# Two transformer blocks in one kernel: the triangular inverse masked after its products and turned out of PSUM, and the output gates as seven quarter products

## The chip, the cores and the metric

One core of a Trainium2 chip, float32 throughout. The metric is the device time in microseconds of one execution. The program is written for the engines directly: each of TensorE (PE), VectorE (DVE), ScalarE (ACT), GpSimd (POOL) and SyncE (SP, which issues the loads) has a list of its own, in an order written out by hand, and waits on counters that the other engines raise.

## The reference

x is 256 tokens of 1024 channels. Block 1 (a mixer of four branches and a gated feed-forward) is not touched. Block 2 projects its normalised input and computes, per channel pair-block of 128,

```python
c_val, c_gate, c_og, ts, r_og, g_conv, g_rwkv = jnp.split(p, SPLITS, axis=-1)
y_conv = _conv_branch(c_val, c_gate, c_og, ...)
y_rwkv = _rwkv7_branch(ts, r_og, ...)
m = jax.nn.sigmoid(g_conv) * y_conv + jax.nn.sigmoid(g_rwkv) * y_rwkv
```

The recurrent branch is a scan over tokens, sixteen heads of 64 channels:

```python
sk = jnp.einsum('bhvk,bhk->bhv', state, kk_t)
state = (state * w_t[:, :, None, :] - sk[..., None] * b_t[:, :, None, :]
         + v_t[..., None] * k_t[:, :, None, :])
return state, jnp.einsum('bhvk,bhk->bhv', state, r_t)
```

The kernel does it in four chunks of 64 tokens. Within a chunk it needs the inverse of a unit triangular 64x64 matrix, I + N, per head and chunk.

## The kernel before

**Stages.** The heads of block 2 come in eight pairs (128 channels, two heads). For each pair j there are nine projections of 8 matmuls, 128x128 weights against 256 columns of `hT`, the block's input with channels on partitions (`projection`, L972): VAL, GATE, K, R, V for the pair after (list NEXT) and OGP, ROG, GCP, GRP for the pair itself (list OWN). GCP and GRP are the logits of the two output gates, `g_conv` and `g_rwkv`.

**Order on PE.** `pe_rwkv(e, j)` (j from 0 to 8) interleaves three things: the chain of pair j-1 over its four chunks (`forced` L1064/L1066, `solved` L1074, `outcome` L1087 to L1101), the triangular inverse of pair j (`grown` L1116, `inverted` L1128/L1130), and between these a fixed number of projection steps, `fill(next(n))`, out of the generator `behind`. One step is one matmul; FILL = (0, 12, 11, 12, 11, 13, 13) holds for pairs 1 to 6, with 72 steps for the 9 projections of 8. The fills are shorter in pair 7 (FILL_LAST) and behind it (FILL_END).

**Banks.** Projections alternate between the left halves of banks 0 and 1, in the order of list ORDER. Before projection n starts, `read_out` waits until projection n-2 has been read: by ACT's `hv`, `cth`, `own.*`, `gc`, `gr`, or by DVE's `og`, `rg`.

**The inverse.** It is built up by levels l = 0 to 5, of blocks of 2 to the l. PE multiplies B and A into bank 2 (L947), ACT copies the product to `Nt` (L1650). POOL (`pool_rwkv`) masks it into Z0 (L2894), adds the unit (L2896), and writes five masked copies `Nm`, one for each of the levels 1 to 5 (L2892). DVE transposes Z0 into Xs (L2455). At level l PE forms Nm_l times Xs (`grown`), DVE adds the unit on the way out of bank 2 (L2449), PE multiplies Z by that into bank 3 (`inverted`), ACT copies half of the columns into Xs (L1633), and DVE transposes Xs into Zs:

```python
e.wait_ge(*(act.upto(f"X{l}.{j}") if l else pool.upto(f"Z0.{j}")))
to, of, name = (Zs[j % 2], Xs, "Z") if l else (Xs, Zs[j % 2], "X")
e.transpose(flat(to), flat(of)).then_inc(*dve.step(f"{name}{l}.{j}"))
```

**Order on DVE.** `dve_rwkv(e, j)` starts with `forced(0)` (copy F0 out of bank 7, L2431), `solved(0)` (copy U0, L2435) and the bonus product (L2480). Then come taps of the depthwise convolution (L2389: 31 for each pair, spread over two pairs), the transpose of Z0, more taps, `state(1)` (St1, L2442), `grown(1)`, and so on. PE's `forced(1)` (L1064) waits for St1. At the pair's end stand `rg_silu` (L2467), `operand_r` (L2369), `group_norm` and taps of the next pair; then `forced(0)` of the next pair waits for PE (L1066).

**Order on ACT.** `act_rwkv(e, j)`: copies of Nt and of the tokens' values (L1651), then value, gate and operand copies as their projections finish, X copies between them, tanh for the low rank (L1553), exponentials, a square root with a table load, and at the pair's end the group norm's copies and `half_gate` (L1642): tanh of half of the logits, out of the bank into GC[:, j, :] and GR[:, j, :].

**Loads.** SP's list loads a slot of 512 KB for each projection: for pair j first NEXT of j+1, then OWN of j, each behind the product that last read that slot. The last stage's early weights go to slots 9 to 11.

**Elsewhere.** Block 1's gates and the feed-forward already use seven quarter products in place of eight (Winograd's scheme): `quarter_product` (L819), four sums of weights (L1925 to L1931), four of the tokens' quarters (`quarter_sums`, L2120 to L2125), and sums on the way out (L1937 to L1948).

Of the kernel before, what the change touches and what calls it, by code (L numbers as in the profile page):

```python
# [49 lines left out]
def columns(*fields):  # L50
    at, out = 0, {}
    for name, n in fields:
# [14 lines left out]
                      ("off_first", CHUNK), ("off", LEVELS * CHUNK), ("centre", CHUNK), ("unit", CHUNK),  # L67
                      ("up", CHUNK), ("st", CHUNK), ("upper_chunks", P), ("cmask", P))
NKEPT = CCOL["onehot"]
NFIRST = CCOL["off_first"]  # L70


def shape_constants():
# [14 lines left out]
    put("off_first", (i == t + 1) & (i % 2 == 1))  # L88
    for l in range(LEVELS):
        n = 1 << l  # L90
        c[:, CCOL["off"] + l * CHUNK:CCOL["off"] + (l + 1) * CHUNK] = \
            (i // (2 * n) == t // (2 * n)) & (i // n % 2 == 0) & (t // n % 2 == 1)
# [55 lines left out]
def build(nc, a, out):  # L148

    with ExitStack() as ctx:  # L150
# [227 lines left out]
        Nm = carve((LEVELS - 1) * CHUNKS, CHUNK)  # L378
# [8 lines left out]
        mid = cst[:, CCOL["mid"]:CCOL["mid"] + 3]  # L387

# [567 lines left out]
        def read_out(e, n):  # L956

            if n >= 0:
                w, q = ORDER[n]
                if w in (OGP, ROG, LNSUM, LNVAR):  # L960
# [5 lines left out]
        def projection(e, w, q):  # L966
# [4 lines left out]
            for k in range(KT):  # L971
# [3 lines left out]
                yield  # L975

# [52 lines left out]
        def behind(e, j):  # L1029

            if j < LAST:
                for w in NEXT:
                    yield from projection(e, w, j + 1)
                for w in OWN:
                    yield from projection(e, w, j)
            elif j == LAST:
# [10 lines left out]
        def pe_rwkv(e, j):  # L1047
# [56 lines left out]
            def grown(l):  # L1104

                if l == 1:
                    e.wait_ge(*pool.upto(f"Nm1.{j}"))
                    e.wait_ge(*dve.upto(f"X0.{j}"))
                    e.wait_ge(*act.upto(f"tokV.{j}"))
                else:  # L1110
                    e.wait_ge(*pool.upto(f"Nm{l}.{j}"))
# [515 lines left out]
        def act_rwkv(e, j):  # L1627
# [3 lines left out]
            def inverted(l):  # L1631
                e.wait_ge(*pe.upto(f"XZ{l}.{j}"))
# [792 lines left out]
        def dve_rwkv(e, j):  # L2425
# [21 lines left out]
            def grown(l):  # L2447
                e.wait_ge(*pe.upto(f"G{l}.{j}"))
                e.tensor_tensor(Gs, chunks(half(2)), each(cst2_of("unit")), ALU.add).then_inc(*dve.step(f"G{l}.{j}"))  # L2449

            def turned(l):

                e.wait_ge(*(act.upto(f"X{l}.{j}") if l else pool.upto(f"Z0.{j}")))
                to, of, name = (Zs[j % 2], Xs, "Z") if l else (Xs, Zs[j % 2], "X")
                e.transpose(flat(to), flat(of)).then_inc(*dve.step(f"{name}{l}.{j}"))  # L2455
# [12 lines left out]


            if chain:  # L2470
                forced(0)
# [790 lines left out]
```

## Time and profile before

| what | value |
|---|---|
| median of 3 runs | 1079.8 us (1078.93 to 1079.96) |
| the profiled execution | 1079.88 us, span 1078.1 us |
| granted clock of PE | 0.999 |
| PE busy | 1065.6 us, 99% |
| DVE busy | 720.0 us, 67% |
| ACT, POOL busy | 235.3 us, 149.7 us |
| read from HBM | 160.73 MB |

The span is the time from the first to the last instruction of the profiled execution; its own time is that execution's device time, and what lies between the two is before and behind the instructions. Times in rows are microseconds from the start of the span unless marked ns. "Idle before, releaser" says how long an engine stood still before a group of instructions and what ended it. A float32 matmul of the program stands in the trace as two PE instructions. Starts of consecutive DVE instructions can lie closer together than their durations.

### The profile page before, as it was taken

The numbers are of one execution on the slowest core, as the hardware profiler recorded it, in microseconds if no ns is written. First come the engines' busy times: TensorE is split into PE (matmuls) and PEld (weight loads), VectorE is DVE, ScalarE is ACT, GpSimd is POOL, SyncE is SP. The second block draws the span as 40 slices with busy tenths as digits, with TensorE's granted clock in tenths as the row PEclk, the third lists the DMA queues.
The fourth block names the chain that finished last, engine by engine and source line by source line (L and its number), as shares of the span: only waits on it lengthen the run. The fifth ranks groups of instructions, "written<-read, shape, count | busy, mean of one in ns | idle before, by whom it ended". The sixth has DMA issues, their size and how long they took to land.

```text
span 1078.1 us, 21003 instructions
## 1 busy us (share of the span) xinstructions
PE 1065.6 (99%) x8606; PEld 910.8 (84%) x8606; DVE 720.0 (67%) x1624; ACT 235.3 (22%) x614; POOL 149.7 (14%) x204
## 2 busy tenths in 40 slices
PE   9999999999999999999999999999999999999997
PEld 7899899998998589999744988888888888887983
DVE  4476674766744377777657768666667667666885
ACT  4131130312210020010101422323232232323101
POOL 1101000000036221100160022020202202020042
PEclk9999999999999999999999999999999999999999
DMA  8676566553347346555446233233332322161251
GB/s 286 236 274 250 188 213 215 161 196 98 138 144 262 124 135 215 193 189 182 168 170 259 79 117 99 89 108 99 99 104 94 111 87 80 27 249 40 79 157 40
DMA packets 62769, 163.20 MB, mean 151 GB/s; under 512 B 8625, under 2 KB 22865, under 8 KB 62674
## 3 DMA queue, kind: packets, MB, share of 16 engines
q1 hardware_dynamic: 61666, 160.22, 44.7%
q8 instruction: 69, 1.13, 0.4%
q10 hardware_dynamic: 1008, 1.63, 0.4%
q14 instruction: 26, 0.21, 0.1%
HBM read 160.73 MB, written 1.11 MB: 150 GB/s over the span
## 4 chain that ended last, share of the span: by engine, by line
PE 91%; DVE 6%; DMA 2%; issue 1%; ACT 0%; DVEq 0%; ACTq 0%
PE bank L819 22%; PE bank L972 20%; PE bank L471 16%; PE bank L885 6%; DVE arena L2389 3%; PE bank L631 3%; PE bank L751 2%; PE bank L794 2%; PE bank L1128 2%; PE bank L1285 2%; PE bank L1116 2%; PE bank L1007 1%; PE bank L947 1%; DMA slots<-in_w_br 1%; PE bank L547 1%; PE bank L953 1%
## 5 line engine op out<-in xcount | busy, mean ns | idle before, releaser
L972 PE MATMUL bank<-hT,slots 128*128 128x256 f32 x1120 | 254.6, 382 | 0.0
L972 PEld LDWEIGHTS bank<-hT,slots 128*128 128x128 f32 x1120 | 209.8, 190 | 28.8
L471 PE MATMUL bank<-hT,slots 128*128 128x256 f32 x544 | 119.7, 379 | 0.0
L471 PEld LDWEIGHTS bank<-hT,slots 128*128 128x128 f32 x544 | 103.0, 190 | 14.4 <-issue 0.6
L2389 DVE SCALAR_TENSOR_TENSOR arena<-padA,par,arena 128x256 f32<-128x256 f32 x232 | 113.9, 552 | 0.0
L819 PE MATMUL bank<-arena,slots 128*128 128x128 f32 x768 | 95.6, 275 | 0.0
L819 PE MATMUL bank<-hT,slots 128*128 128x128 f32 x736 | 91.8, 276 | 0.2 <-DVE arena L1937 0.2
L819 PEld LDWEIGHTS bank<-arena,slots 128*128 128x128 f32 x768 | 90.9, 192 | 0.5
L819 PEld LDWEIGHTS bank<-hT,slots 128*128 128x128 f32 x736 | 86.7, 192 | 1.1 <-issue 1.1
L471 PE MATMUL bank<-arena,slots 128*128 128x256 f32 x304 | 66.5, 380 | 0.5 <-DMA slots<-in_w_br 0.5
L471 PEld LDWEIGHTS bank<-arena,slots 128*128 128x128 f32 x304 | 57.5, 190 | 9.0 <-DMA slots<-in_w_br 1.3
L885 PE MATMUL bank<-slots,arena 128*128 128x512 f32 x128 | 55.4, 592 | 0.0
L2894 POOL TENSOR_TENSOR arena<-arena 128x256 f32<-128x256 f32 x8 | 5.8, 729 | 343.4 <-ACT arena L1650 343.4
L885 PEld LDWEIGHTS bank<-slots,arena 128*128 128x128 f32 x128 | 24.2, 190 | 30.1 <-issue 25.6
L2455 DVE STREAM_TRANSPOSE arena<-arena 128x256 f32<-128x256 f32 x40 | 17.7, 442 | 35.8 <-ACT arena L1633 35.0
L1858 DVE TENSOR_SCALAR arena<-bank 64x256 f32<-64x256 f32 x24 | 10.1, 422 | 38.3 <-PE bank L471 37.9
L2892 POOL TENSOR_TENSOR arena<-arena 128x256 f32<-128x256 f32 x40 | 34.3, 888 | 0.0
L819 PE MATMUL bank<-x,slots 128*128 128x128 f32 x256 | 33.9, 275 | 0.1
L819 PE MATMUL bank<-x,arena 128*128 128x128 f32 x256 | 33.8, 275 | 0.0
L819 PEld LDWEIGHTS bank<-x,slots 128*128 128x128 f32 x256 | 31.2, 192 | 0.3 <-DVE arena L1948 0.3
L819 PEld LDWEIGHTS bank<-x,arena 128*128 128x128 f32 x256 | 31.2, 192 | 0.0
L1902 DVE SCALAR_TENSOR_TENSOR adaA<-arena,sc,adaA 128x1024 f32<-128x1024 f32 x24 | 30.7, 1279 | 0.1
(449 smaller groups left out, 1741.3 us busy)
## 6 DMA issues: line engine op xcount, KB each, us to landing
slots<-in_w_rwkv SPq DMA_DIRECT2D x72, 512.0 KB, 3.6
slots<-in_w_heads SPq DMA_DIRECT2D x68, 512.0 KB, 4.5
slots<-in_w_gu SPq DMA_DIRECT2D x44, 512.0 KB, 4.5
arena<-in_ada_w SPq DMA_DIRECT2D x24, 512.0 KB, 5.4
slots<-in_w_down SPq DMA_DIRECT2D x20, 512.0 KB, 4.3
slots<-in_w_br SPq DMA_DIRECT2D x32, 256.0 KB, 2.8
slots<-in_w_out SPq DMA_DIRECT2D x16, 512.0 KB, 4.1
slots<-in_w_y SPq DMA_DIRECT2D x16, 512.0 KB, 5.2
```

What stands on the lines that cost most here:

```text
L471: end = e.matmul(psum, w[:, k * P:(k + 1) * P], rhs[:, k, :], start=k == 0, stop=k == kt - 1)
L631: end = e.matmul(view3(bank[5][:, t * T:(t + 1) * T], P), hT[:, k, t * P:(t + 1) * P], slots[:, BV:CV + 1, k * P:(k + 1) * P], start=k == ...
L751: return e.matmul(bank[DOWN_BANK[m]][:, :], *sides, start=j == 0, stop=j == OUT_PAIRS - 1)
L794: end = e.matmul(psum[:, tokens(t)], w[:, k * P:(k + 1) * P], hT[:, k, tokens(t)], start=k == 0, stop=k == KT - 1)
L819: end = e.matmul(out, w[:, k * P:(k + 1) * P], rhs[:, k, :], start=k == 0, stop=k == 3)
L885: return e.matmul(bank[DOWN_BANK[m]][:, :], *sides, start=j == 0, stop=j == DOWN - 1)
L972: end = e.matmul(proj(w, q), slot[w][:, k * P:(k + 1) * P], hT[:, k, :], start=k == 0, stop=k == KT - 1)
L1116: end = e.matmul(bank[2][r, c * CHUNK:(c + 1) * CHUNK], Nm[r, (l - 1) * CHUNKS + c, :], Xs[r, c, :], start=True, stop=True)
L1128: end = e.matmul(chunks(half(3))[r, c, :], Z[r, c, :], Gs[r, c, :], start=True, stop=True)
L1902: e.scalar_tensor_tensor(out=third, in0=adaW[n % 2], scalar=sc[:, 2 * i + n // 3:2 * i + n // 3 + 1], in1=third, op0=ALU.mult, op1=ALU.add ...
L2389: e.scalar_tensor_tensor(out=o, in0=src, scalar=w, in1=o, op0=ALU.mult, op1=ALU.add).then_inc(*dve.step(f"tap{n}.{q}"))
L2892: e.tensor_tensor(Nm[:, (l - 1) * CHUNKS:l * CHUNKS, :], Nt, each(cst2_of("off", CHUNK, l * CHUNK)), ALU.mult).then_inc(*pool.step(f"Nm{l} ...
```

## The change

1. **Masks.** POOL no longer makes `Nm`. It keeps the strict triangle of Nt, adds the unit in place (Nd), and masks the first level into Z0. PE's `grown(l)` multiplies the whole Nt with Xs at each level, and DVE's instruction on the way out multiplies with the level's mask (which holds the unit) where it added the unit. The constants change with it.
2. **Transposes.** DVE transposes Z_l straight out of bank 3 when PE has the product; ACT's copy to Xs waits for that transpose.
3. **Gates.** For pairs 1 to 6, GCP and GRP become `own_gate_pair`: 28 matmuls of 128 columns, in 14 steps of two. Four weight sums stand in DVE's list behind transposes 1, 2 (two of them) and 4. ACT copies the first quarter's product, DVE adds the others (`first_quarter` at the pair's end, `other_quarters` in the next pair behind F0), and ACT applies tanh in place at the start of the next pair. Pair 0 and pair 7 stay plain.
4. **Tokens' sums.** `quarter_sums` for block 2 stand behind pair 0's last taps.
5. **Loads.** Slot GCP is loaded behind the last product of GRP; the early output weights behind GRP of pair 6, since slots 9 to 11 hold the sums.

```diff
@@ tiles
-        Nm = carve((LEVELS - 1) * CHUNKS, CHUNK)
+        bt = [slot[9 + n // 2][:, n % 2 * 512:(n % 2 + 1) * 512].rearrange("p (k n) -> p k n", n=P) for n in range(4)]
+        bs = [slot[11][:, 0:512], slot[11][:, 512:], adaA[:, 2 * D:2 * D + 512]]
@@ read_out
+                if w in (GCP, GRP) and 0 < q < LAST:
+                    e.wait_ge(*dve.upto(f"bq11.{q}" if w == GCP else f"bq1221.{q}"))
@@ PE
+        def own_gate_pair(e, q):
+            one, two = gate_banks_of(q)
+            low, high = hT[:, 0:4, :], hT[:, 4:8, :]
+            first, second = (slot[w] for w in (GCP, GRP))
+            parts = ((one, 0, first[:, 0:512], low[:, :, tokens(0)]), (one, 1, first[:, 512:], high[:, :, tokens(0)]), (one, 2, bs[0], bt[1]),
+                     (two, 0, second[:, 0:512], bt[0]), (two, 1, bs[1], bt[2]), (two, 2, bs[2], high[:, :, tokens(1)]), (two, 3, second[:, 512:], bt[3]))
+            for n, (out, at, w, rhs) in enumerate(parts):
+                if n == 0:
+                    e.wait_ge(*in_slot[GCP].upto(f"rw{GCP}.{q}"))
+                    read_out(e, PLACE[GCP, q] - 2)
+                if n == 2:
+                    e.wait_ge(*dve.upto("bt4"))
+                    e.wait_ge(*dve.upto(f"bs4.{q}"))
+                if n == 3:
+                    read_out(e, PLACE[GRP, q] - 2)
+                for k in range(4):
+                    end = e.matmul(out[:, at, :], w[:, k * P:(k + 1) * P], rhs[:, k, :], start=k == 0, stop=k == 3)
+                    if k == 3 and n in (2, 6):
+                        end.then_inc(*pe.step(f"b126.{q}" if n == 2 else f"p{GRP}.{q}"))
+                    if k % 2:
+                        yield
@@ PE, grown(l)
-                    e.wait_ge(*pool.upto(f"Nm1.{j}"))
+                    e.wait_ge(*pool.upto(f"Nd.{j}"))
-                        end = e.matmul(bank[2][r, c * CHUNK:(c + 1) * CHUNK], Nm[r, (l - 1) * CHUNKS + c, :], Xs[r, c, :], start=True, stop=True)
+                        end = e.matmul(bank[2][r, c * CHUNK:(c + 1) * CHUNK], Nt[r, c, :], Xs[r, c, :], start=True, stop=True)
@@ ACT
             def inverted(l):
-                e.wait_ge(*pe.upto(f"XZ{l}.{j}"))
+                e.wait_ge(*dve.upto(f"Z{l}.{j}"))
...
-                if j:
-                    e.wait_ge(*pool.upto(f"Nm{LEVELS - 1}.{j - 1}"))
...
+            if levels and j > 1:
+                for w, to in (("gc", GC[:, p, :]), ("gr", GR[:, p, :])):
+                    e.wait_ge(*dve.upto(f"bq1221.{p}"))
+                    e.activation(to, to, ACT.Tanh, scale=0.5).then_inc(*act.step(f"{w}.{p}"))
...
-                half_gate(GCP, GC[:, j, :], "gc", j)
+                if more and chain:
+                    e.wait_ge(*pe.upto(f"b126.{j}"))
+                    e.activation(GC[:, j, P:], gate_banks_of(j)[0][:, 0, :], ACT.Copy).then_inc(*act.step(f"bp1.{j}"))
+                else:
+                    half_gate(GCP, GC[:, j, :], "gc", j)
                 if more:
-                    half_gate(GRP, GR[:, j, :], "gr", j)
+                    if not chain:
+                        half_gate(GRP, GR[:, j, :], "gr", j)
@@ DVE
-                e.tensor_tensor(Gs, chunks(half(2)), each(cst2_of("unit")), ALU.add).then_inc(*dve.step(f"G{l}.{j}"))
+                e.tensor_tensor(Gs, chunks(half(2)), each(cst2_of("within", CHUNK, (l - 1) * CHUNK)), ALU.mult).then_inc(*dve.step(f"G{l}.{j}"))
...
+                if l:
+                    e.wait_ge(*pe.upto(f"XZ{l}.{j}"))
+                    e.transpose(flat(Zs[j % 2]), half(3)).then_inc(*dve.step(f"Z{l}.{j}"))
...
+            def slice_sum(k):
+                a11, a12, a21, a22 = (slot[s][:, columns_half(h)] for s in (GCP, GRP) for h in range(2))
+                if k == 0:
+                    e.wait_ge(*in_slot[GCP].upto(f"rw{GCP}.{j}"))
+                    e.wait_ge(*in_slot[GRP].upto(f"rw{GRP}.{j}"))
+                    e.tensor_tensor(bs[1], a11, a21, ALU.subtract).then_inc(*dve.step(f"bs3.{j}"))
...
+            def first_quarter(q):
+                e.wait_ge(*act.upto(f"bp1.{q}"))
+                e.tensor_tensor(own_gates(q, 0), GC[:, q, P:].unsqueeze(1).to_broadcast([P, 2, P]), gate_banks_of(q)[0][:, 1:3, :],
+                                ALU.add).then_inc(*dve.step(f"bq11.{q}"))
...
+            def other_quarters(q):
...
             if chain:
                 forced(0)
+            if levels and j > 1:
+                other_quarters(p)
...
                 turned(1)
+            if more and chain:
+                slice_sum(0)
...
                 turned(2)
+            if more and chain:
+                slice_sum(1)
+                slice_sum(2)
...
                 turned(4)
+            if more and chain:
+                slice_sum(3)
...
                 taps(e, j + 1, 13 if chain else 10, 18)
+            if j == 0:
+                quarter_sums(e, bt, "bt", (act.upto("norm4.s3.1"), dve.upto("norm4.s7.1"), pe.upto("lora")))
+            elif more:
+                first_quarter(j)
@@ POOL
-            e.tensor_tensor(Zs[j % 2], Nt, each(cst2_of("off")), ALU.mult).then_inc(*pool.step(f"Z0.m.{j}"))
-            e.wait_ge(*pool.upto(f"Z0.m.{j}"))
-            e.tensor_tensor(Zs[j % 2], Zs[j % 2], each(cst2_of("unit")), ALU.add).then_inc(*pool.step(f"Z0.{j}"))
-            blocks(1)
-            for l in range(2, LEVELS):
-                blocks(l)
+            e.tensor_tensor(Nt, Nt, each(cst2_of("st")), ALU.mult).then_inc(*pool.step(f"Nd.m.{j}"))
+            e.wait_ge(*pool.upto(f"Nd.m.{j}"))
+            e.tensor_tensor(Nt, Nt, each(cst2_of("unit")), ALU.add).then_inc(*pool.step(f"Nd.{j}"))
+            e.wait_ge(*pool.upto(f"Nd.{j}"))
+            e.tensor_tensor(Zs[j % 2], Nt, each(cst2_of("first")), ALU.mult).then_inc(*pool.step(f"Z0.{j}"))
@@ SP
-                e.wait_ge(*pe.upto(f"p{w}.{j - 1}" if j else free[w]))
+                e.wait_ge(*pe.upto(f"p{GRP if w == GCP else w}.{j - 1}" if j else free[w]))
...
-            e.wait_ge(*pe.upto("lora"))
+            e.wait_ge(*pe.upto(f"p{GRP}.{LAST - 1}"))
```

## Rows read from the trace of the kernel before

**Rows 1.** The page: engines' busy times, and the issues of block 2's projection loads.

```profile
PE 1065.6 (99%) x8606; PEld 910.8 (84%) x8606; DVE 720.0 (67%) x1624; ACT 235.3 (22%) x614; POOL 149.7 (14%) x204
...
slots<-in_w_rwkv SPq DMA_DIRECT2D x72, 512.0 KB, 3.6
```

**Rows 2.** Windows, one period of five: length; busy PE, weight loads, DVE, ACT, POOL; clock; DMA.

```profile
745.30:793.20 47.90, 47.52 (x545) 41.24 (x545) 33.88 (x78) 13.59 (x34) 5.94 (x7) 1.00 0.33 101
```

**Rows 3.** Waits of PE over the whole span: total us, times, longest.

```profile
PE bank L1064 <- DVE arena L2442: 2.3, 6, 0.4
```

**Rows 4.** The chain of waits, 793 to 842 us: start, us, what.

```profile
808.79 0.42 DVE arena L2480
...
811.70 3.91 DVE arena L2389 x6
...
823.51 0.47 PE bank L947 x16
```

**Rows 5.** Timeline, 806 to 824 us, PE: start, us, engine, line, operation, idle before.

```profile
814.84 0.63 PE L947 MATMUL bank<-arena 64*64 64x64 f32 x16
...
815.86 0.33 PE L1064 MATMUL bank<-arena 64*64 64x64 f32 x4 [0.38 <-DVE arena L2442]
```

**Rows 6.** The same timeline, DVE and POOL.

```profile
808.17 0.23 DVE L2435 COPY arena<-bank 128x64 f32<-128x64 f32 x1 [0.82 <-PE bank L1074]
...
808.51 0.73 POOL L2894 TENSOR_TENSOR arena<-arena 128x256 f32<-128x256 f32 x1 [41.89 <-ACT arena L1650]
...
808.79 0.42 DVE L2480 TENSOR_TENSOR arena<-arena,bank 128x256 f32<-128x256 f32 x1 [0.39 <-PE bank L1160]
809.13 2.22 DVE L2389 SCALAR_TENSOR_TENSOR arena<-padA,par,arena 128x256 f32<-128x256 f32 x3
...
810.15 4.38 POOL L2892 TENSOR_TENSOR arena<-arena 128x256 f32<-128x256 f32 x5
811.27 0.43 DVE L2455 STREAM_TRANSPOSE arena<-arena 128x256 f32<-128x256 f32 x1
811.63 3.98 DVE L2389 SCALAR_TENSOR_TENSOR arena<-padA,par,arena 128x256 f32<-128x256 f32 x6
...
818.70 1.67 DVE L2389 SCALAR_TENSOR_TENSOR arena<-padA,par,arena 128x256 f32<-128x256 f32 x4
```

**Rows 7.** The chain of waits from 600 us on, two unbroken runs of PE.

```profile
615.39 9.50 PE bank L972 x44
...
1013.20 18.92 PE bank L819 x168
```

**Rows 8.** Groups by line, 1013.3 to 1032 us: products and weight loads: busy us, mean ns.

```profile
L819 PE MATMUL bank<-arena,slots 128*128 128x128 f32 x96 | 11.9, 275 | 0.0
...
L819 PEld LDWEIGHTS bank<-arena,slots 128*128 128x128 f32 x94 | 11.1, 192 | 0.1
```

**Rows 9.** Timeline of DVE, 952 to 956 us (pair 7).

```profile
954.12 0.43 DVE L2455 STREAM_TRANSPOSE arena<-arena 128x256 f32<-128x256 f32 x1
```

**Rows 10.** Waits of DVE, 697.4 to 937 us: total us, times, longest.

```profile
DVE arena L2455 <- ACT arena L1633: 25.5, 15, 2.8
...
DVE arena L2324 <- ACT arena L1553: 3.6, 5, 0.7
```

**Rows 11.** Groups by line, DVE, 697.4 to 937 us: count, busy us, mean ns.

```profile
L2352 DVE RECIPROCAL arena<-arena 128x256 f32<-128x256 f32 x5 | 8.8, 1754 | 0.2
```

**Rows 12.** Groups by line, DVE, 180 to 260 us (block 1's sums of the same kinds).

```profile
L1925 DVE TENSOR_TENSOR arena<-slots 128x512 f32<-128x512 f32 x5 | 3.4, 689 | 0.1
...
L1946 DVE TENSOR_TENSOR arena<-arena,bank 128x128 f32<-128x128 f32 x4 | 1.1, 288 | 0.1
```

**Rows 13.** Groups by line, DVE, 390 to 394 us (block 1's tokens' sums).

```profile
L2121 DVE TENSOR_TENSOR arena<-hT 128x512 f32<-128x512 f32 x1 | 0.7, 686 | 0.0
```

**Rows 14.** Timeline, 662 to 666 us, DVE and PE (pair 0 to pair 1).

```profile
663.82 0.23 DVE L2431 COPY arena<-bank 128x64 f32<-128x64 f32 x1 [0.66 <-PE bank L1066]
...
664.54 0.28 PE L1074 MATMUL bank<-arena 64*64 64x64 f32 x4
```

More of the change, by code:

```diff
@@ L66 @@
                       ("onehot", 3 * P), ("gmask", 3 * P),
[L67 removed]
+                      ("first", CHUNK), ("within", (LEVELS - 1) * CHUNK), ("centre", CHUNK), ("unit", CHUNK),
                       ("up", CHUNK), ("st", CHUNK), ("upper_chunks", P), ("cmask", P))
 NKEPT = CCOL["onehot"]
[L70 removed]
+NFIRST = CCOL["first"]
 def shape_constants():
@@ L87, in shape_constants @@
     i, t = r % CHUNK, np.arange(CHUNK)[None, :]
-    put("off_first", (i == t + 1) & (i % 2 == 1))
-    for l in range(LEVELS):
+    put("first", (i == t) | (i == t - 1) & (t % 2 == 1))
+    for l in range(1, LEVELS):
         n = 1 << l
-        c[:, CCOL["off"] + l * CHUNK:CCOL["off"] + (l + 1) * CHUNK] = \
-            (i // (2 * n) == t // (2 * n)) & (i // n % 2 == 0) & (t // n % 2 == 1)
+        at = CCOL["within"] + (l - 1) * CHUNK
+        c[:, at:at + CHUNK] = (i == t) | (i // (2 * n) == t // (2 * n)) & (t // n % 2 == 0) & (i // n % 2 == 1)
     put("unit", i == t)
@@ L975, in projection, with gate_banks_of @@
                 yield
+        def gate_banks_of(q):
+            return [view3(bank[PLACE[w, q] % 2][:, :], P) for w in (GCP, GRP)]
+        def own_gate_pair(e, q):
[19 more added lines that the diff above has]
+                        yield
         def layer_sum(e, w, src):
@@ L1033, in behind @@
                     yield from projection(e, w, j + 1)
-                for w in OWN:
+                for w in (OGP, ROG) if j else OWN:
                     yield from projection(e, w, j)
+                if j:
+                    yield from own_gate_pair(e, j)
             elif j == LAST:
@@ L2467, in rg_silu @@
                 e.scalar_tensor_tensor(out=rg[j % 3], in0=rg[j % 3], scalar=1.0, in1=proj(ROG, j), op0=ALU.add, op1=ALU.mult).then_inc(*dve.step(f"rg.{j}"))
+            def slice_sum(k):
[4 more added lines that the diff above has]
+                    e.tensor_tensor(bs[1], a11, a21, ALU.subtract).then_inc(*dve.step(f"bs3.{j}"))
+                elif k == 1:
+                    e.wait_ge(*dve.upto(f"bs3.{j}"))
+                    e.tensor_tensor(a21, a21, a22, ALU.add).then_inc(*dve.step(f"bs1.{j}"))
+                elif k == 2:
+                    e.wait_ge(*dve.upto(f"bs1.{j}"))
+                    e.tensor_tensor(bs[0], a21, a11, ALU.subtract).then_inc(*dve.step(f"bs2.{j}"))
+                else:
+                    e.wait_ge(*dve.upto(f"bs2.{j}"))
+                    e.tensor_tensor(bs[2], a12, bs[0], ALU.subtract).then_inc(*dve.step(f"bs4.{j}"))
+            def first_quarter(q):
[3 more added lines that the diff above has]
+            def other_quarters(q):
+                two = gate_banks_of(q)[1]
+                e.wait_ge(*pe.upto(f"p{GRP}.{q}"))
+                e.wait_ge(*dve.upto(f"bq11.{q}"))
+                e.tensor_tensor(own_gates(q, 1), GR[:, q, P:].unsqueeze(1).to_broadcast([P, 2, P]), two[:, 0:2, :],
+                                ALU.add).then_inc(*dve.step(f"bu43.{q}"))
+                e.wait_ge(*dve.upto(f"bu43.{q}"))
+                e.tensor_tensor(GR[:, q, P:], GR[:, q, 0:P], two[:, 0, :], ALU.add).then_inc(*dve.step(f"bq22.{q}"))
+                e.wait_ge(*dve.upto(f"bq22.{q}"))
+                e.tensor_tensor(own_gates(q, 1), own_gates(q, 1), two[:, 2:4, :], ALU.add).then_inc(*dve.step(f"bq1221.{q}"))
             if chain:
                 forced(0)
+            if levels and j > 1:
+                other_quarters(p)
             if end:
```

16 lines of the change are left out of this document (7 added, 9 removed).

## The prediction

> **What bounds the kernel now.** I read the page first: TensorE (PE) is busy 1065.6 of 1078.1 us, VectorE (DVE) 67% [rows 1]. Then the windows, one for each pair of heads of block 2: pairs 2 to 6 have periods of 47.9 or 48.0 us from 697.4 us on, PE busy 47.5 of each, DVE 31 to 34, GpSimd (POOL) 5.9, granted clock 1.00, the full level [rows 2]. So time is won only where PE has less to stream or waits less. PE's waits name one group in block 2: L1064 for DVE, 6 times, 2.3 us in all [rows 3]. The chain of waits shows why. Behind the bonus product it leaves PE and runs through DVE's bonus (L2480), three taps, the transpose and six taps to St1 (L2442), and comes back to PE at 815.86 [rows 4]. PE could have come sooner: a group of 16 L947 products lasts 0.47 us on the chain where nothing holds it up [rows 4], and the one before this L1064 began at 814.84 [rows 5]. Allowing 0.46 to 0.47, 815.86 - 814.84 - 0.46 = 0.56 us are lost in each such pair.
>
> DVE is late there through POOL: three taps take 2.22 us and six take 3.98 while POOL works, from 808.51 to 814.53; four taps elsewhere take 1.67 [rows 6]. That is up to 0.87 a tap, about a POOL instruction's length, against 0.41. The transpose keeps its 0.43 beside POOL.
>
> **The change, part by part.**
>
> *Quarter products.* Each e.matmul is two PE instructions (560 calls of L972, 1120 records). The two gates of a pair now are 32 instructions of 256 columns, and then 56 of 128. In unbroken runs on the chain 44 of the former take 9.50 us, 0.216 each, and 168 of the latter 18.92, 0.1126 each [rows 7]. 32 x 0.216 - 56 x 0.1126 = 6.91 - 6.31 = 0.60 us a pair, times six pairs (1 to 6) is 3.6 us, all on PE. Busy times alone, 11.9 us for 96 records, give 0.124 each and no saving [rows 8]; I take the chain, since it holds the pace of the stream. Bounds 0 and 3.9 (0.64 a pair, at 0.112). The fill list stays, so the last gap of a pair has 11 steps instead of 13 and the saving falls there.
>
> *Masks behind the products.* POOL loses five instructions of 0.88 us (4.38 in all) and gains one: 7 become 3, about 2.5 us instead of 6.0 [rows 6]. DVE's mask multiply takes the place of an addition of the same shape: nothing. Z0 is the third POOL instruction now, ready near 808.51 + 2.55 = 811.06, and DVE reaches the transpose at 811.27 [rows 6]: nothing in pairs 1 to 6. In pair 7 DVE comes at 954.12 [rows 9]; POOL, as late against the pair's start as elsewhere, gives Z0 near 954.8. The 0.7 us are paid back by two taps at 0.41 that are slowed now, and PE comes for St1 some 0.3 after DVE has it: nothing, with 0.3 as its bound. In pairs 1 to 6 the six taps come free of POOL, 6 x 0.41 = 2.5 instead of 3.9, so DVE could begin St1 near 814.2; its product S0 is there about 814.3. The 0.56 us of PE goes: 6 x 0.56 = 3.4 us. Bounds: 2.3 (the waits view) and 3.5. Late next is G1, near 815.3, just when PE gets to it.
>
> *Inverses turned from the bank.* DVE waits for ACT ahead of its transposes, 15 times in five periods, 25.5 us in all, 2.8 at most [rows 10]: 5.1 us a pair. It now waits for PE's product, and ACT's X copy waits for DVE instead. Behind that copy in ACT's queue stand lw.tanh (ACT waits for PE there anyway), the decays, the square root's table, and og.th; behind them kk_lengths and og_silu on DVE. PE waits for X only behind a whole fill. On the path: nothing, while a transpose out of a bank costs about what it costs in SBUF. That is not in the trace. From below 0.42, an addition of this size out of a bank [rows 4]; from above 1.75 us, DVE's dearest instruction on 256 columns [rows 11]. I take 0.44, since its own SBUF row is 0.43 and a bank operand leaves other instructions of this size at 0.42.
>
> *Slice sums.* Four of 0.69 us, each dependent on the last [rows 12]: 2.9 us on DVE a pair. Three stand right behind transposes, in the 5.1 us just freed: one where DVE waited for ACT and again for lw.tanh (0.7 at most [rows 10]), two, 1.45 us, where the wait of 2.8 was, one ahead of og_silu. All hidden; if that cover goes, F2's copy behind the two is the first to be late. They wait for both slots. SyncE loads slot GCP now behind the pair's last product (GRP's), near 806, with GRP's load right behind; before, GCP's went when its own product was done, 3.4 us earlier. A load lands in 3.6 us [rows 1]; two in a row by 813.5, and DVE asks at 817.4. The later loads of the queue stood behind GRP's wait already.
>
> *Sums of the quarters.* first_quarter, 0.42 us, waits for ACT's one copy and goes where DVE idles before F0. The other three, 0.42, 0.29 and 0.42 in a dependent row of 1.2 us [rows 12], stand between F0 and U0, where DVE idles 0.82, and 0.39 more ahead of the bonus [rows 6]. U0 comes 0.2 late, the bonus on time. PE's VAL waits for bq11, done before it; GATE for bq1221, due 3.5 us later. ACT's two tanh move to the pair's start, where it waits for PE's next projection: nothing.
>
> *Tokens' sums.* Four DVE instructions behind pair 0's last tap, which ends at 663.17: starts 0.61, 0.60 and 0.72 apart, 0.69 long [rows 13], to 665.75. F0's copy stood at 663.82, with 0.66 idle ahead, and PE's solved(0), which waits for it, at 664.54 [rows 14]. The copy now ends near 665.95 and PE stands still 1.4 us. Nothing takes it back. Below 1.2; above 2.0, if POOL slows one or two of them.
>
> *Rest.* The three early output loads stood behind GRP's last load in the queue already; the constants are 64 columns fewer: nothing. Behind pair 6 the waits of PE name nothing in block 2 [rows 3], so what is won before passes to the end.
>
> **Sum.** The profiled execution took 1079.88 us (span 1078.1, the rest around it); the median shown, 1079.8, is 0.08 less. 1079.88 - 3.6 - 3.4 + 1.4 = 1074.3 us rounded up.
>
> **The rivals.** Measurement can tell about 0.2%, 2.2 us, from no change.
> - *The stall stays* (12%). The three sums ahead of U0 eat what POOL gives back, or the stall is PE's own. For it: DVE has no idle time from 808.79 to 815.72. Against: 1.4 us comes back there, 0.1 goes. Only the products pay: 1079.88 - 3.6 + 1.4 = 1077.7.
> - *The products save nothing* (6%). 56 records at the busy times' 0.124 us are 6.94 us, as before: 1079.88 - 3.4 + 1.4 = 1077.9.
> - *DVE becomes late, slower* (6%). A transpose out of the bank at 1.75 us puts 1.3 us on each of four a pair. F2's copy has no idle ahead of it now, and the two slice sums stand just before: some 1.2 us a pair reach PE, my estimate from 1.3 + 1.45 - 2.8 at that place and 1.3 without cover at the next transpose, and about 4 us in pair 7, whose fills are half as long. 1074.3 + 6 x 1.2 + 4 = 1085.5. It decides from about 1.1 us a transpose.
> - *The weights' loads come out* (2%). A load row is 192 ns long, though 94 of them share 11.1 us, 0.118 each [rows 8]. If one had to end before the next begins, 56 x 0.192 = 10.75 us a pair against 6.91: 1079.88 + 6 x 3.84 - 3.4 + 1.4 = 1100.9. The Trainium skill (TensorE: Matmul & The Clock Gate, Part 3, The mechanism) says that a load overlaps running products only where the row group differs, which speaks for this rival. The trace does not agree: the unbroken run at 0.1126 has full 128-row weights.
> - *More comes* (4%). Tokens' sums find cover I don't see: 1072.9.
>
> **How the numbers follow.** The forecast has 70%; its own range goes from 1079.88 - 3.9 - 3.5 + 1.2 = 1073.7 to 1079.88 - 3.6 - 2.3 + 2.0 + 0.3 = 1076.3. The whole range, 1073.0 to 1077.8, takes in the first rival and most of the last. Faster by over 0.2%: 70 + 4 + half of the first rival = 80%. Within: its other half, the second and a little of the third, 13%. Slower: 7%.
>
> **What would show it.** Right: windows of about 46.7 us for pairs 2 to 6, L1064 gone from PE's waits, POOL 2.5 us a pair, six taps in 2.5 us behind the first transpose, no ACT wait ahead of transposes, one new PE wait of 1.4 us at solved(0) near 664.5. Wrong: transposes over 0.6 us, L1128 or L1074 waiting for DVE in every pair, quarter products over 0.12 us apart, DVE waiting at its first slice sum for a load.

## The result and the profile after

The changed kernel takes 1072.87 us (median of 4 runs, 1071.67 to 1073.36), the kernel before 1079.37 us beside it (4 runs, 1078.37 to 1079.96). The ratio is 0.9938, with an interval of [0.9925, 0.9951]: faster by 0.6%. The forecast was 1074.3 us with a range from 1073.0 to 1077.8, so the direction was right and the time lies 0.13 us below the range. The places of the gains and of the one new wait are the ones forecast; what was too small were the two gains. The profiled execution took 1073.22 us, its span is 1071.4 us.

The page of the changed kernel, busy times [rows 1]:

```profile
PE 1060.8 (99%) x8750; PEld 914.3 (85%) x8750; DVE 735.5 (69%) x1676; ACT 235.3 (22%) x620; POOL 123.2 (12%) x172
```

Windows of the changed kernel, with the columns of [rows 2]: pair 2, pairs 6 and 7 on to the end, and then all from pair 0's first POOL instruction to the end; a window begins with the first POOL instruction of its pair:

```profile
712.64:759.24 46.60, 46.60 (x570) 41.66 (x569) 36.45 (x87) 13.60 (x36) 2.39 (x3) 1.00 0.34 105
...
899.05:945.66 46.61, 46.61 (x570) 41.66 (x569) 36.45 (x87) 13.60 (x36) 2.39 (x4) 1.00 0.15 47
945.66:1071.40 125.74, 118.54 (x976) 94.12 (x974) 92.08 (x193) 25.61 (x57) 24.39 (x25) 0.99 0.36 117
...
626.18:1071.40 445.22, 436.51 (x4791) 376.00 (x4789) 338.34 (x777) 119.40 (x294) 41.15 (x46) 1.00 0.32 99
```

The last of these windows in the kernel before:

```profile
626.54:1078.10 451.56, 441.81 (x4647) 373.52 (x4645) 322.57 (x725) 119.41 (x288) 68.71 (x78) 1.00 0.32 98
```

A pair takes 46.60 us instead of 47.91, and PE is now busy for all of it. What lies from pair 0 to the end is 6.34 us shorter. POOL's share of a pair fell from 5.94 to 2.39 us. DVE has 2.6 us more to do in a pair (36.45 against 33.88), and PE waits for it nowhere in pairs 2 to 6. From pair 7 to the end the kernel before takes 125.86 us.

PE's waits over the whole span of the changed kernel: the group of [rows 3] is gone, and the one new group was forecast, once, at solved(0) of pair 1:

```profile
PE bank L1114 <- DVE arena L2477: 1.3, 1, 1.3
PE bank L511 <- POOL padA L2900: 1.2, 1, 1.2
PE bank L480 <- DMA slots<-in_w_br: 0.5, 1, 0.5
```

The chain of waits of the changed kernel, 799 to 815 us. Where it left PE for DVE in [rows 4], it now stays on PE (L1104/L1106 are forced, L1167 is inverted, L1009 the quarter products):

```profile
799.03 5.11 PE bank L1009 x44
804.14 0.26 PE bank L1106 x4
...
812.81 0.12 PE bank L1104 x4
812.92 0.12 PE bank L1106 x4
813.04 0.60 PE bank L1167 x16
```

The timeline of DVE in the same pair, which answers to [rows 6]: transpose of Z0, six taps, St1, and then the transpose out of the bank with the first slice sum right behind it:

```profile
808.60 0.43 DVE L2504 STREAM_TRANSPOSE arena<-arena 128x256 f32<-128x256 f32 x1
808.96 2.42 DVE L2435 SCALAR_TENSOR_TENSOR arena<-padA,par,arena 128x256 f32<-128x256 f32 x6
811.69 0.28 DVE L2488 TENSOR_SCALAR arena<-bank,arena 128x64 f32<-128x64 f32 x1 [0.32 <-PE bank L1129]
...
813.68 0.45 DVE L2501 STREAM_TRANSPOSE arena<-bank 128x256 f32<-128x256 f32 x1
814.05 0.65 DVE L2524 TENSOR_TENSOR slots<-slots 128x512 f32<-128x512 f32 x1
```

Six taps take 2.42 us instead of 3.98, and DVE idles 0.32 us ahead of St1 where it had been the late one. Of DVE's waits ahead of transposes, 25.5 us for ACT in [rows 10], there is left, in the same stretch of 697.4 to 937 us, one group for PE's product, and no wait of DVE there is for a load:

```profile
DVE arena L2501 <- PE bank L1167: 4.4, 11, 0.5
```

### The profile page after: what moved, and what is told of

The parts are those of the page before. It is cut to its first block, busy times and chain, and to the rows that moved or that the text cites. A ratio compares the mean times of both kernels' runs of the same rounds, so it can differ in the third digit from the quotient of the medians.

```text
span 1071.4 us, 21316 instructions
## 1 busy us (share of the span) xinstructions
PE 1060.8 (99%) x8750; PEld 914.3 (85%) x8750; DVE 735.5 (69%) x1676; ACT 235.3 (22%) x620; POOL 123.2 (12%) x172
## 4 chain that ended last, share of the span: by engine, by line
PE 97%; DVE 1%; DMA 1%; issue 0%; ACT 0%; POOL 0%; DVEq 0%; ACTq 0%; POOLq 0%
PE bank L828 23%; PE bank L983 19%; PE bank L480 17%; PE bank L894 6%; PE bank L1009 4%; PE bank L640 3%; PE bank L760 2%; PE bank L803 2%; PE bank L1155 2%; PE bank L1167 2%; PE bank L1324 2%; PE bank L1045 1%; PE bank L956 1%; PE bank L556 1%; PE bank L962 1%; PE bank L511 1%
## 5 line engine op out<-in xcount | busy, mean ns | idle before, releaser
L983 PE MATMUL bank<-hT,slots 128*128 128x256 f32 x928 | 211.7, 382 | 0.0
L983 PEld LDWEIGHTS bank<-hT,slots 128*128 128x128 f32 x928 | 173.7, 190 | 24.1 <-issue 0.3
L480 PE MATMUL bank<-hT,slots 128*128 128x256 f32 x544 | 119.7, 379 | 0.0
L480 PEld LDWEIGHTS bank<-hT,slots 128*128 128x128 f32 x544 | 103.0, 190 | 14.4 <-issue 0.6
L2435 DVE SCALAR_TENSOR_TENSOR arena<-padA,par,arena 128x256 f32<-128x256 f32 x232 | 102.3, 502 | 0.0
L828 PEld LDWEIGHTS bank<-hT,slots 128*128 128x128 f32 x736 | 86.7, 192 | 0.9 <-issue 0.9
L2984 POOL TENSOR_TENSOR arena<-arena 128x256 f32<-128x256 f32 x8 | 6.2, 772 | 361.0 <-ACT arena L1687 361.0
L1556 ACT ACTIVATE arena<-bank 128x128 f32<-128x128 f32 x20 | 5.6, 278 | 110.0 <-PE bank L828 104.8
L640 PE MATMUL bank<-slots,hT 128*128 128x256 f32 x128 | 28.9, 379 | 0.0
```

The lines of the kernel that those rows point to most:

```text
L480: end = e.matmul(psum, w[:, k * P:(k + 1) * P], rhs[:, k, :], start=k == 0, stop=k == kt - 1)
L640: end = e.matmul(view3(bank[5][:, t * T:(t + 1) * T], P), hT[:, k, t * P:(t + 1) * P], slots[:, BV:CV + 1, k * P:(k + 1) * P], start=k == ...
L828: end = e.matmul(out, w[:, k * P:(k + 1) * P], rhs[:, k, :], start=k == 0, stop=k == 3)
L983: end = e.matmul(proj(w, q), slot[w][:, k * P:(k + 1) * P], hT[:, k, :], start=k == 0, stop=k == KT - 1)
L2435: e.scalar_tensor_tensor(out=o, in0=src, scalar=w, in1=o, op0=ALU.mult, op1=ALU.add).then_inc(*dve.step(f"tap{n}.{q}"))
```

## The experiments

All medians stand beside runs of the kernel before on the same chip: 1079.37 us for the changed kernel, 1079.02 for plain gates, old masks, old transposes and tokens' sums first, 1079.07 for the changed kernel once more, old masks late, gates alone and pair 0 by quarters, 1078.98 for the other four. Effects under 1 us are read from the traces, since the pair periods repeat to 0.02 us from one execution to the next. "Block 2" is the time from pair 0's first POOL instruction to the end.

| kernel | period, us | block 2, us | median, us | ratio, interval |
|---|---|---|---|---|
| before | 47.91 | 451.6 | 1079.37 | |
| changed | 46.60 | 445.2 | 1072.87 | 0.9938 [0.9925, 0.9951] |
| changed, once more | 46.60 | 445.3 | 1072.68 | 0.9940 [0.9927, 0.9952] |
| plain gates | 47.26 | 447.7 | 1075.91 | 0.9965 [0.9953, 0.9978] |
| old masks | 47.25 | 448.5 | 1076.51 | 0.9974 [0.9963, 0.9985] |
| old transposes | 47.64 | 451.4 | 1078.55 | 0.9995 [0.9987, 1.0004] |
| transposes alone | 47.92 | 451.7 | 1079.42 | 1.0003 [0.9994, 1.0011] |
| gates alone | 48.30 | 454.7 | 1082.76 | 1.0031 [1.0020, 1.0043] |
| old masks, late | 46.60 | 445.3 | 1073.94 | 0.9949 [0.9936, 0.9961] |
| old masks, later | 47.30 | 449.4 | 1076.78 | 0.9978 [0.9969, 0.9987] |
| tokens' sums first | 46.60 | 443.8 | 1071.08 | 0.9927 [0.9913, 0.9940] |
| the same, once more | 46.60 | 443.8 | 1071.56 | 0.9930 [0.9918, 0.9943] |
| and pair 0 by quarters | 46.60 | 444.5 | 1072.18 | 0.9936 [0.9922, 0.9949] |
| and rg_silu sooner | 46.61 | 443.3 | 1070.61 | 0.9921 [0.9908, 0.9935] |

**Plain gates.** The gates of pairs 1 to 6 as in the kernel before, masks and transposes as changed.

```diff
-                for w in (OGP, ROG) if j else OWN:
+                for w in OWN:
                     yield from projection(e, w, j)
-                if j:
-                    yield from own_gate_pair(e, j)
```

> Masks and transposes as changed; the output gates of pairs 1 to 6 as eight plain products again, so no slice sums, no sums of the quarters and no tokens' sums. My theory (two gains and one cost add up): against the changed kernel it loses the products (6 x 0.66 = 4.0 us, by the two chains) and gets the 1.4 us of pair 0 to 1 back, so about 1072.9 + 4.0 - 1.4 = 1075.5 us, 3.9 below the kernel before (1079.4), with PE's wait at forced(1) gone and a period of 47.25 us. Rival 1 (the stall left because PE's order of fills changed, not because of POOL): the wait at forced(1) is there again, about 1079.4. Rival 2 (products save nothing, something else does): period 46.6 as in the changed kernel and about 1071.5.

Measured: 1075.91 us, no wait of PE in block 2. Pair 6 in its windows:

```profile
852.39:899.65 47.26, 47.26 (x546) 41.22 (x545) 32.78 (x78) 13.45 (x35) 2.39 (x3) 1.00 0.32 102
```

The period is 0.66 us longer than the changed kernel's, in each of the pairs 2 to 6, and PE is busy for all of it in both. The products save 0.66 us a pair, and nothing else in the gates' part touches PE but the tokens' sums: 6 x 0.66 - 1.48 = 2.5 us, which is what block 2 is longer by.

**Old masks.** POOL makes its five copies again, the rest as changed.

```diff
-            e.tensor_tensor(Zs[j % 2], Nt, each(cst2_of("first")), ALU.mult).then_inc(*pool.step(f"Z0.{j}"))
...
+            for l in range(1, LEVELS):
+                blocks(l)
...
-                        end = e.matmul(bank[2][r, c * CHUNK:(c + 1) * CHUNK], Nt[r, c, :], Xs[r, c, :], start=True, stop=True)
+                        end = e.matmul(bank[2][r, c * CHUNK:(c + 1) * CHUNK], Nm[r, (l - 1) * CHUNKS + c, :], Xs[r, c, :], start=True, stop=True)
```

> The changed kernel, but POOL makes the five masked copies again (seven instructions a pair instead of three) and DVE adds the unit; transposes, quarter products and sums stay as changed. My theory (POOL's instructions slow DVE's taps, and these make St1 late): six taps take 3.9 us again instead of 2.4, PE waits for St1 at forced(1) in each of pairs 1 to 6 or a little more than before, since three sums stand ahead of U0: 6 x 0.65 = 3.9 us, about 1076.8 us, period 47.25. Rival (the stall was due to the transposes or the order, not to POOL): as the changed kernel, 1072.9, no wait at forced(1).

Measured: 1076.51 us. The stall is back. PE's waits from 606 us on, and the chain, 806 to 817 us:

```profile
PE bank L1105 <- DVE arena L2492: 1.9, 5, 0.4
PE bank L1115 <- DVE arena L2481: 1.3, 1, 1.3
```

```profile
809.17 2.13 DVE arena L2439 x3
811.30 0.35 DVE arena L2508
811.65 3.90 DVE arena L2439 x6
815.56 0.21 DVE arena L2492
...
815.80 0.33 PE bank L1105 x4
816.14 0.12 PE bank L1107 x4
816.25 0.66 PE bank L1169 x16
```

It is the chain of [rows 4] again, with the same length of six taps. It comes five times and not six: in pair 1 the tokens' sums have made PE late already, and that pair takes 47.65 or 47.66 us with either set of masks: there one delay hides the other. The row of inverted(1), 0.66 us against 0.60 in the changed kernel, is the second, small part of the stall.

**Old masks, late.** As before it, but copies 2 to 5 wait for St1.

```diff
             for l in range(1, LEVELS):
+                if l == 2 and j:
+                    e.wait_ge(*dve.upto(f"St1.{j - 1}"))
                 blocks(l)
```

> As the run with POOL's five masked copies, but copies 2 to 5 wait until DVE has made St1; so POOL does as much in all, and three of its instructions stand beside DVE's taps, as in the changed kernel. My theory (what costs is a POOL instruction beside DVE's taps ahead of St1, not POOL's load): the stall at forced(1) goes, period 46.6 to 46.7, about 1073 us. Rival 1 (POOL's load slows DVE wherever it stands, and PE pays anyway): period 47.25, 1076.5. Rival 2 (the copies come too late for grown(2) or slow what DVE does behind St1, and G1 or the first transpose is late): a new PE wait behind forced(1), up to 0.9 us a pair, 1078.

Measured: 1073.94 us, periods of 46.60, PE's waits those of the changed kernel. Pair 6 in its windows:

```profile
853.15:899.75 46.60, 46.60 (x570) 41.65 (x569) 36.46 (x87) 13.60 (x36) 5.71 (x7) 1.00 0.32 103
```

POOL works 5.71 us here against 2.39 in the changed kernel, and a pair is just as long. It is the place of POOL's work that cost 0.65 us, not its amount. The median is 1.3 us above that of the changed kernel once more, which ran on the same chip. Block 2 takes 445.33 us in both traces, and the traced execution begins pair 0 at 626.87 us where the other has 624.97, so what differs lies ahead of block 2's pairs.

**Old masks, later.** Copies 2 to 5 wait for the first slice sum instead (`bs3`), so that they fall beside four taps that follow it.

> As the run with copies 2 to 5 behind St1, but they wait for the first slice sum, so that POOL works beside DVE's four taps there. My theory (a POOL instruction holds up DVE's taps and hardly anything else of DVE): four taps take about 3 us instead of 1.67, DVE's wait ahead of grown(2) (several tenths of a us) takes it up, and PE loses little: period 46.6 to 46.9, 1074 to 1075 us. Rival (only the taps behind the first transpose are sensitive, by what lies in their place): four taps at 1.67 still, period 46.6, 1073.9 us.

Measured: 1076.78 us, period 47.30. The direction of my expectation held and its size didn't. DVE's timeline, and PE's waits from 606 us on:

```profile
817.07 0.49 DVE L2374 TENSOR_SCALAR arena<-arena 128x256 f32<-128x256 f32 x1 [0.47 <-ACT arena L1594]
817.48 3.08 DVE L2439 SCALAR_TENSOR_TENSOR arena<-padA,par,arena 128x256 f32<-128x256 f32 x4
...
822.77 0.22 DVE L2485 COPY arena<-bank 128x64 f32<-128x64 f32 x1
```

```profile
PE bank L1128 <- DVE arena L2485: 2.9, 6, 0.5
```

The four taps take 3.08 us instead of 1.67 and the scaling ahead of them 0.49 instead of 0.29: 1.6 us in all. In the changed kernel DVE idles only 0.43 us ahead of the copy of U1 that follows, so this copy comes 1.1 us later against St1 (9.18 us behind it instead of 8.09). PE needs it at L1128, 0.6 us after the old copy was done, and stands 0.5. And L1128's group, behind a wait, takes 0.33 us where the changed kernel's takes 0.12. That makes the 0.70 of the period. I had set the delay against the wait ahead of grown(2) and missed that U1's copy stands before it.

**Old transposes.** Each transpose waits for ACT's copy and reads that.

```diff
-                    e.wait_ge(*pe.upto(f"XZ{l}.{j}"))
-                    e.transpose(flat(Zs[j % 2]), half(3)).then_inc(*dve.step(f"Z{l}.{j}"))
+                    e.wait_ge(*act.upto(f"X{l}.{j}"))
+                    e.transpose(flat(Zs[j % 2]), flat(Xs)).then_inc(*dve.step(f"Z{l}.{j}"))
```

> The changed kernel, but each transpose waits for ACT's copy and reads that, as before. My theory (the slice sums are hidden only because the 5.1 us of waiting are gone): DVE gets 2.9 us of slice sums on top of waits it had, F2's copy and what follows come 1.0 to 1.4 us late in each of pairs 1 to 6, and PE waits for DVE there: 1072.9 + 6 to 9 = about 1080 us, with a new group of PE waits for F2 or the transposes in all pairs. Rival (DVE has room enough in any case, the new transposes only make it quieter): within 1 us of the changed kernel, 1072.9, and no new wait on PE.

Measured: 1078.55 us, period 47.64, which is 1.04 more in each of pairs 2 to 6 and 1.01 in pair 1, 6.2 us in block 2. DVE's timeline at the place that the prediction named (L2477 is F2's copy, L2527 and L2530 the two slice sums), and then PE's:

```profile
778.51 0.45 DVE L2501 STREAM_TRANSPOSE arena<-arena 128x256 f32<-128x256 f32 x1 [2.78 <-ACT arena L1672]
778.88 0.65 DVE L2527 TENSOR_TENSOR slots<-slots 128x512 f32<-128x512 f32 x1
779.57 0.69 DVE L2530 TENSOR_TENSOR slots<-slots 128x512 f32<-128x512 f32 x1
...
783.81 0.22 DVE L2477 COPY arena<-bank 128x64 f32<-128x64 f32 x1
```

```profile
784.08 0.33 PE L1114 MATMUL bank<-arena 64*64 64x64 f32 x4 [0.73 <-DVE arena L2477]
```

The wait of 2.78 us for ACT is back, the sums stand behind it, and F2's copy follows with no idle time. ACT is not slow there: its X copy stands in its list behind two copies of a projection (L1631, L1633), and PE finishes that projection only at 777.31 us. PE pays 0.73 us of waiting, 0.21 because the group behind the wait takes 0.33 us instead of 0.12, and 0.06 in the group after it. In the changed kernel this transpose waits 0.53 us for PE and F2's copy has 0.63 us to spare. Without the transposes out of the bank the whole change would have been worth nothing that can be measured: 0.9995, with an interval over 1, and block 2 of 451.4 us against 451.6.

**Transposes alone**, on the masks and gates of the kernel before.

> The transposes out of the bank alone: masks, gates and sums as in the kernel before. My theory (they only give DVE room, nothing on PE's path waited for it): period 47.91 us as before, 1079.0 to 1079.4 us, the ratio's interval over 1.000, and DVE with some 5 us a pair less of waits ahead of transposes. Rival (the earlier transpose itself lets PE come sooner): period under 47.8, 1078 us or less.

Measured: 1079.42 us, 1.0003, period 47.91 or 47.92. DVE's longest group of waits in [rows 10], for ACT ahead of the transposes, is gone, and PE waits for St1 as before:

```profile
PE bank L1101 <- DVE arena L2480: 2.3, 6, 0.4
```

So the part that the change can't do without brings nothing by itself.

**Gates alone**, on the old masks and the old transposes.

> The gates by quarters alone, with the tokens' sums where the change has them: masks and transposes as in the kernel before. My theory (the parts need each other: 1.04 us a pair for the slice sums without cover, 0.65 for POOL, 0.66 saved, at different places of the pair, so that they add): period 47.91 - 0.66 + 1.04 = 48.29, that is 1078.6 + 6 x 0.65 = 1082.4 us, slower than the kernel before by 0.3%. Rival (one DVE delay hides the other, since PE waits only once for the same lateness): period 47.7 to 47.9, 1079 to 1080 us.

Measured: 1082.76 us, and a period of 48.30 = 47.91 - 0.66 + 1.04. PE's waits from 606 us on show the delay of F2's copy in six pairs and the tokens' sums once (the first row), and St1's delay in five:

```profile
PE bank L1115 <- DVE arena L2481: 5.7, 7, 1.3
PE bank L1105 <- DVE arena L2492: 1.9, 5, 0.4
```

They add, since they lie in different places of the pair. The quarter products alone are a slower kernel.

**Tokens' sums first.** The four sums move from behind pair 0's last taps to the front of pair 0's bonus.

```diff
         def dve_first(e):
...
             operand_r(e, 0)
+            quarter_sums(e, bt, "bt", (act.upto("norm4.s3.1"), dve.upto("norm4.s7.1"), pe.upto("lora")))
...
-            if j == 0:
-                quarter_sums(e, bt, "bt", (act.upto("norm4.s3.1"), dve.upto("norm4.s7.1"), pe.upto("lora")))
```

> The changed kernel, but the four tokens' sums stand before pair 0's bonus, where DVE is idle for 3.9 us, instead of behind pair 0's last taps. My theory (the sums make solved(0) of pair 1 late and nothing takes it back): PE's wait there goes and the whole kernel is 1.4 us shorter, 1071.4 us. Rival 1 (the time is taken back somewhere later, or another wait takes its place): 1072.9, and pair 1 as much longer as pair 0 is shorter. Rival 2 (the sums at the new place make pair 0's chain late): 1073 or more, with a PE wait in pair 0.

Measured: 1071.08 us. When it ran again, 1070.9 to 1071.4 us were expected with pair 1 at 46.17; it took 1071.56, a little above that, with pair 1 at 46.17 and block 2 as long to 0.02 us. Its pair 1 in the windows takes 46.18 us, where the changed kernel's takes 47.65:

```profile
664.29:710.47 46.18, 46.18 (x568) 41.28 (x567) 33.44 (x82) 12.74 (x33) 2.39 (x4) 1.00 0.33 105
```

Pair 0 keeps its 38.80 us and no other period moves. DVE still idles 1.35 us ahead of the bonus. So the changed kernel had the sums at the wrong place: the 1.4 us that they cost were there to be had.

**Pair 0 by quarters too.**

> Tokens' sums before pair 0's bonus, as in the run before, and the output gates of pair 0 by quarters too. My theory (each pair by quarters saves PE 0.66 us, whatever pair it is): 1071.1 - 0.7 = 1070.4 us, pair 0 to 1 at 38.2 us instead of 38.8. Rival 1 (pair 0's fills are other than those of pairs 1 to 6, and DVE has its slice sums in the way there): 1071.1 or above, with a PE wait in pair 0. Both lie within what five runs can tell, so the length of pair 0 decides.

Measured: 1072.18 us, and pair 0 takes 38.98 us, 0.18 more instead of 0.66 less. PE's waits from 606 us on:

```profile
PE bank L1009 <- DVE arena L2513: 0.7, 1, 0.7
PE bank L1166 <- issue: 0.2, 1, 0.2
```

L2513 is `rg_silu`, which must have read its bank before the second product of the gates begins. By quarters the first product is 0.8 us shorter (24 instructions in 2.68 us on the chain, against 16 of 0.216), so the second one comes sooner than DVE is done. That is rival 1. The rest of the loss is 0.45 us in pair 7, at an L1166 group, with "issue" for its releaser. No other run has it, and its cause stays open.

**And rg_silu sooner.** In pair 0 it stands ahead of the taps that precede grown(5).

```diff
                 if not chain:
-                    taps(e, j + 1, 6, 10)
+                    rg_silu()
+                    taps(e, j + 1, 6, 9)
...
-                rg_silu()
+                if chain:
+                    rg_silu()
```

> All seven pairs 0 to 6 by quarters, tokens' sums before pair 0's bonus, and in pair 0 rg_silu ahead of three taps, since PE waited 0.7 us for it before GRP's first quarter in the earlier run. My theory: that wait goes, pair 0 to 1 takes 38.98 - 0.8 = 38.2 us, and the time is 1071.1 - 0.66 = 1070.4 us. Rival (the next late thing takes its place: the last slice sum or grown(5)): pair 0 to 1 at 38.6 or more, 1070.9 us or more.

Measured: 1070.61 us. Pair 0 takes 38.19 us, PE waits for nothing from 606 us on, and this is the fastest of all: 0.8% below the kernel before, 2.3 us below the changed one. Pair 0 is 0.61 us shorter than with its plain gates, but pair 1 takes 46.27 us instead of 46.17, 0.10 of it at solved(0), for which F0's copy is now only just in time. Block 2 is 0.5 us shorter, where 0.66 was expected.

**The changed kernel once more.**

> The changed kernel once more, on the chip of these three. If the difference between the executions lies in block 1 alone, which no part of the change touches: pair periods of 46.60 us again to 0.02, 125.8 us from pair 7 to the end, the first POOL instruction of pair 0 anywhere from 625.0 to 627.5 us, and a median from 1072 to 1073.5 us. If it lies in block 2, the periods differ.

Measured: 1072.68 us, periods of 46.60 or 46.61, pair 1 at 47.66. Its pair 0 begins at 624.97 us, the changed kernel's first trace has 626.18.

## Why the prediction was right, and where it fell short

**The products: right, mis-sized.** I took 0.60 us a pair from runs of 44 and 168 instructions; it is 0.66. The chain of the run with the transposes alone, whose gates are those of before, has the two last fills of the pair as

```profile
791.33 5.81 PE bank L982 x26
...
799.12 5.81 PE bank L982 x26
```

At the long run's 0.216 us, 26 instructions are 5.61 us, so each fill costs 0.20 us more than its pace. By quarters the last fill is 5.11 us for 44, and 44 x 0.1126 = 4.95, so the same is 0.16 there. In these traces a fill that begins behind small products pays for its beginning, and pays less with 128 columns. That makes 0.04 of the missing 0.06. The other 0.02 is in the fill ahead of it, which holds 20 instructions of plain products and 12 of the quarters:

```profile
791.20 4.51 PE bank L983 x20
795.71 1.34 PE bank L1009 x12
```

Its pace would make it 0.06 us longer than 26 plain ones, and it is 0.04 longer, 5.85 against 5.81; why is open. The long runs of [rows 7] had hidden all this, and my upper bound of 0.64 from the same runs was below the truth (0.64 times six is 3.8 besides, not the 3.9 that I wrote).

**The loads.** In the fill of 5.11 us the weight loads are 192 ns long each and the products come 0.116 us apart:

```profile
L1009 PEld LDWEIGHTS bank<-slots 128*128 128x128 f32 x32 | 3.7, 192 | 0.0
```

So they overlap with full 128-row weights, and the rival had it wrong. The rule of the Trainium skill that the prediction weighed (TensorE: Matmul & The Clock Gate, Part 3, The mechanism), that a load overlaps running products only where the row group differs, does not agree with this trace. The same section also says that a load into the background weight buffer is pulled ahead of running products; the 0.116 us fit that, and no run here shows which buffer was used.

**The stall: right, mis-sized.** I had 0.56 us at forced(1), and the runs with old masks show 0.65 a pair. The step from the transposes alone to plain gates, which differ in the masks only, says the same: block 2 goes from 451.68 to 447.73 us, 3.95 for six pairs. Inside one pair the path from forced(0) to inverted(1) is 0.59 us longer in the run with old masks, and inverted(1) itself 0.06. The 0.59 are the wait of 0.37 us and some 0.21 in which the group behind it is slower (0.33 us on the chain instead of 0.12). The 0.06 I had not looked for: when St1 is late, G1 behind it is late as well, which I had put down as "late next" without a price.

**POOL as its cause: right.** Two runs with the same copies at two places, which differ in that one wait, settle it: one at 46.60 and one at 47.25. The rival that the stall was PE's own is refuted.

**The transposes: right.** Out of the bank they take 0.44 to 0.45 us, the estimate was 0.44. Alone they make block 2 0.12 us longer, where I had put nothing: pair 0 takes 38.81 us instead of 38.68, in one fill of 12 instructions (2.71 us instead of 2.59). Every trace that has them shows it and no other does; its cause stays open. What I wrote of the cover, that F2's copy is the first to be late, is what the run with the old ones shows, with 1.04 us a pair.

**The tokens' sums: right.** The stall was forecast at 1.4 us and is 1.48 (47.65 - 46.17). That nothing takes it back was right too, though with the old masks they cost only 0.85 (47.66 against 47.47 - 0.66), since they hide pair 1's other stall.

**The loads of the slots, sums of quarters, taps of pair 7: nothing, as forecast.** DVE waits for no load ahead of its slice sums, and from pair 7 to the end it is 125.74 us, 125.86 before, with 125.74 to 125.88 in all traces but one.

**The sum.** Block 2 is 6.34 us shorter, where the terms gave 3.4 + 3.6 - 1.4 = 5.6. Three kernels in a row split it: from the kernel before to the transposes alone block 2 gets 0.12 us longer (forecast nothing), from there to plain gates 3.95 shorter (forecast 3.4), and from there to the changed kernel 2.51 shorter (forecast 3.6 - 1.4 = 2.2). The profiled execution lies 1.1 us below the forecast: these 0.74, and 0.36 us of block 1, where nothing was changed. The median lies 0.35 lower still.

**The range failed** at its low end, and the step that failed is "its own range goes from 1079.88 - 3.9 - 3.5 + 1.2", with two terms that were mis-sized: the products at 0.60 us a pair measured 0.66, and the stall at 0.56 measured 0.65. Both bounds came from the same rows as the values, so they were too near: the true terms, 6 x 0.66 = 3.96 and 6 x 0.65 = 3.9, lie outside of both. With the true sum the forecast would have been 1079.88 - 6.34 = 1073.5 us, below its own range and still inside the whole one. What took the result below 1073.0 as well is the spread between executions, for which no part of the range stood, though the three times shown lay 1.0 us apart: I counted from one execution of 1079.88, and the kernel before had its median at 1079.37 beside the changed one.

**A rival with the right number.** "More comes" gives 1072.9 us, which the result meets to 0.03, and the range that I said took in most of it stopped 0.1 short of it. But its reason isn't what happened: the tokens' sums found no cover, and PE stood still 1.3 us for them. That the numbers meet is chance.

## What to carry to other kernels

A cycle that repeats gives a gauge of 0.02 us even where whole executions of one kernel differ by 3 us, so read small effects from periods and only then from medians. A piece of work for an idle engine is hidden only behind waits that the change removes at that very place, so ask of each part whether it is a gain or the cover of another, and put work of a second engine where its neighbour runs instructions that don't collide with it. A pace taken from a long unbroken run leaves out what each short fill pays to begin.

## What the runs showed of the hardware

**Which DVE instructions suffer from POOL.** Beside POOL's copies a tap (both inputs in SBUF) goes from 0.41 to about 0.8 us apart, and a scaling in SBUF from 0.29 to 0.49, while additions with one operand in a bank stay at 0.42 and transposes at 0.43 to 0.45. It goes the other way too. In the run with copies 2 to 5 behind St1, POOL's copies, 809 to 817 us (minimum, median and longest, in ns):

```profile
L2989 POOL TENSOR_TENSOR arena<-arena x5: 727/730/1182, 808.2 to 814.8; 128x256 f32<-128x256 f32 x5
```

Beside bank reads a copy takes 0.73 us. The last begins 0.06 us behind a slice sum of two SBUF operands, which keeps its 0.65 us, and takes 1.18. In the run with the old masks all five, beside taps, take 0.90 to 0.91. The Trainium skill (SBUF — State Buffer, Who interferes with whom) says that DVE instructions with two SBUF inputs contend with POOL's reads, that those with at most one do not unless they run in a mode that takes both of DVE's ports, as a scaling within SBUF can, and that the later one is blocked until the other is done. The trace agrees for the taps, the additions, the transposes and the slice sum. The scaling, with one SBUF input, was slowed too; whether it ran in such a mode no run here shows. How long the later one is blocked fits only roughly here: the last copy took 0.45 us more than the others, while the slice sum ahead of it had 0.59 us to go.

**Where executions of one kernel differ.** Pair 0 begins at 624.52 us in the earliest trace of the fourteen and at 627.51 in the latest, though no edit touches block 1's instructions. The latest is that with the old masks, whose waits of PE in block 1 hold

```profile
PE bank L481 <- DMA slots<-in_w_br: 0.8, 1, 0.8
PE bank L829 <- DVE arena L1998: 0.3, 1, 0.3
PE bank L829 <- DVE arena L1987: 0.2, 1, 0.2
```

and the run with plain gates, which begins pair 0 at 624.97, has none of these three: they are 1.3 of the 2.5 us between the two. The rest is not accounted for. From 606 us on, PE waits for no load in any of the fourteen traces.
